# A transformer forward pass on one core: three mixer tiles on the unnormed input, and VectorE's convolution work in another order

## The reference

```python
hn = rmsnorm(h, norm_mix_g[l])        # (x * rsqrt(mean(x * x) + 1e-6)) * g
...
z = hn @ w_in                         # 1024 -> 2056 columns
za = jax.nn.gelu(z[..., :o0], approximate=False)
y_a = gmlp_spatial_gating(za[..., :D_A], za[..., D_A:], ln_a_g, ln_a_b, w_s, b_s)
zb = z[..., o0:o1]
y_b = conformer_conv(zb[..., :D_B], zb[..., D_B:], conv_b_w, conv_b_b, gn_b_g, gn_b_b)   # 31 taps
y_c = mlstm_group(z[..., o1:o2], z[..., o2:o3], z[..., o3:o4], z[..., o4:], ...)         # conv of 4 taps, 4 heads
return jnp.concatenate([y_a, y_b, y_c], axis=-1) @ w_out
```

## Time and profile before

| what | value |
|---|---|
| median of 3 runs | 1891.39 us (1889.86 to 1891.47) |
| the profiled execution's own time | 1891.13 us |
| its span, first to last instruction | 1889.3 us |
| PE busy | 1866.1 us |
| PE idle in the first 180 us | 11.4 + 1.1 + 0.7 us |
| mean granted TensorE clock | 0.998 |

### The profile page before, as it was taken

One profiled execution on the slowest core, in us unless ns is written; L12 is line 12 of the kernel. 1 busy time (PEld: TensorE's weight loads), 2 busy tenths in 40 slices (PEclk: granted clock), 3 DMA queues, 4 the chain that ended last, 5 costly groups with the idle time before them and its releaser, 6 DMA issues.

```text
span 1889.3 us, 24381 instructions
## 1 busy us (share of the span) xinstructions
PE 1866.1 (99%) x8998; PEld 1511.8 (80%) x8998; DVE 783.3 (41%) x1278; ACT 433.6 (23%) x846; POOL 1078.6 (57%) x622
## 2 busy tenths in 40 slices
PE   7999999999999999999999999999999999999998
PEld 5878887888888888876778888887877878888887
DVE  6774433352342433687451212127833561212123
ACT  5223422310010122156140101023424140101020
POOL 5755762576757656520556655565862546666652
PEclk9999999999999999999999999999999999999999
DMA  6322321232333224210223332222331223332331
GB/s 228 110 79 90 107 94 45 90 100 90 114 99 112 92 83 146 81 56 1 67 84 96 99 100 89 89 90 89 102 98 46 73 95 101 102 102 95 100 101 45
DMA packets 47455, 173.78 MB, mean 92 GB/s; under 512 B 5264, under 2 KB 5904, under 8 KB 46736
## 3 DMA queue, kind: packets, MB, share of 16 engines
q1 hardware_dynamic: 46800, 169.54, 28.0%
q10 hardware_dynamic: 576, 3.11, 0.5%
HBM read 170.53 MB, written 2.10 MB: 91 GB/s over the span
## 4 chain that ended last, share of the span: by engine, by line
PE 97%; DVE 1%; ACT 1%; DMA 0%; issue 0%; SPq 0%; DVEq 0%
PE acc L516 17%; PE acc L517 17%; PE acc L518 17%; PE acc L543 6%; PE acc L540 6%; PE acc L539 6%; PE acc L595 1%; PE acc L998 1%; PE acc L597 1%; PE acc L596 1%; PE misc L1014 1%; PE misc L1034 1%; PE acc L1190 1%; PE acc L1192 1%; PE acc L1191 1%; PE acc L615 1%
## 5 line engine op out<-in xcount | busy, mean ns | idle before, releaser
L2642 POOL TENSOR_SCALAR w_hi<-raw 128x1024 fp32r<-128x1024 f32 x309 | 335.0, 1084 | 757.9 <-PE acc L543 277.6
L2644 POOL TENSOR_TENSOR w_lo<-raw,w_hi 128x1024 fp32r<-128x1024 f32 x309 | 748.3, 2422 | 25.8
L516 PE MATMUL acc<-x_hi,w_hi 128*128 128x512 f32 x872 | 340.1, 390 | 0.0
L518 PE MATMUL acc<-x_hi,w_lo 128*128 128x512 f32 x872 | 339.3, 389 | 0.0
L517 PE MATMUL acc<-x_lo,w_hi 128*128 128x512 f32 x872 | 339.3, 389 | 0.0
L1970 DVE TENSOR_TENSOR h<-acc,h 128x512 f32<-128x512 f32 x112 | 77.4, 691 | 357.3 <-PE acc L518 226.5
L516 PE MATMUL acc<-y_hi,w_hi 128*128 128x512 f32 x540 | 211.3, 391 | 0.0
L518 PE MATMUL acc<-y_hi,w_lo 128*128 128x512 f32 x540 | 210.1, 389 | 0.0
L517 PE MATMUL acc<-y_lo,w_hi 128*128 128x512 f32 x540 | 210.1, 389 | 0.0
L516 PEld LDWEIGHTS acc<-x_hi,w_hi 128*128 128x128 f32 x872 | 163.7, 188 | 34.2 <-issue 0.3
L518 PEld LDWEIGHTS acc<-x_hi,w_lo 128*128 128x128 f32 x872 | 163.7, 188 | 34.0
(11 more groups left out here) (479 smaller groups left out, 2800.5 us busy)
## 6 DMA issues: line engine op xcount, KB each, us to landing
raw<-weights_dram SPq DMA_DIRECT2D x309, 512.0 KB, 3.5
h<-x_dram SPq DMA_DIRECT2D x2, 1024.0 KB, 6.3
out_dram<-out_tok SPq DMA_DIRECT2D x6, 256.0 KB, 2.1
small<-small_dram SPq DMA_DIRECT2D x1, 1408.0 KB, 15.9
mem_in<-mem_dram SPq DMA_DIRECT2D x1, 1024.0 KB, 13.0
w_cmp<-w_cmp_dram ACTq DMA_DIRECT2D x1, 1024.0 KB, 6.9
small<-small_dram ACTq DMA_DIRECT2D x1, 992.0 KB, 4.8
const<-const_dram SPq DMA_DIRECT2D x1, 640.0 KB, 9.2
```

What stands on the lines that cost most here:

```text
L516: mm(out, m["w_hi"][:, slot, k], hi[:, k], start=k == 0, stop=False)
L518: last = mm(out, m["w_lo"][:, slot, k], hi[:, k], start=False, stop=k == kc - 1)
L2642: nc.gpsimd.tensor_scalar(hi, m["raw"][:, slot], 1.0, 0.0, ALU.mult, ALU.add).then_inc(sem("weights_high"), 1)
L2644: nc.gpsimd.tensor_tensor(m["w_lo"][:, slot].rearrange("p k n -> p (k n)"), m["raw"][:, slot], bf(hi), ALU.subtract).then_inc(sem("weights ...
```

## The change

The first three tiles are now three of the four tiles of `xc`, and the tile of gate rows comes ninth. PE multiplies these three with `x * g`, which needs no norm: ACT writes its high part to `y_hi`, DVE its low part to `y_lo`, and DVE multiplies the finished banks by 1/rms (`r_late`) when it is there (`unnormed_out`). The first tile is split in two halves, and its first four chunks are multiplied before the second half is there. SP brings the first tile and the parameters ahead of x, and x in four pieces. Before that PE runs four products of ones. The sum of squares goes between the chunks of the third tile, behind the writing of `y_hi` and `y_lo` on ACT and DVE. `alpha_b` and `alpha_g` are written later.

DVE does the short convolution, the product of `b_in`, 5 of the 31 taps of the long one, the gate rows and masks, taps 5 to 26, the statistics of the values, two taps, the first head's diagonal, and the last two taps. The norm of the values takes 8 instructions where there were 12. PE takes `conv_mean` after `cell_out(0)` and `gating` after the scores of head 1; the small transposes of the rows stand behind the value tiles. The first head waits for `tile_out` 16 and no more for 17.

```diff
     gates = np.zeros((D, P), np.float32)
     gates[:, 0:4], gates[:, 32:36] = w_in[:, 2048:2052], w_in[:, 2052:2056]
+    for c in [8, 9, 10, 11, 6, 7, 4, 5]:
+        add(w_in, chunk(c))
     add(gates, slice(0, P))
-    for c in [8, 9, 10, 11, 6, 7, 4, 5, 12, 13, 14, 15]:
+    for c in [12, 13, 14, 15]:
         add(w_in, chunk(c))
     add_wide(w_in[:, 256:512], 256)
     for c in (0, 1):
...
-    pe.wait_ge(sem("const_in"), 16)
...
-    idle_products(1)
...
-    idle_products(2)
+    def unnormed(k, slots):
+
+        pe.wait_ge(sem("plain_high"), k + 1)
+        for slot in slots:
+            mm(acc[:, slot], m["w_hi"][:, slot, k], y_hi[:, k], start=k == 0, stop=False)
+            mm(acc[:, slot], m["w_lo"][:, slot, k], y_hi[:, k], start=False, stop=False)
+        pe.wait_ge(sem("plain_low"), k + 1)
+        for slot in slots:
+            last = mm(acc[:, slot], m["w_hi"][:, slot, k], y_lo[:, k], start=False, stop=k == KC - 1)
+            if k == KC - 1:
+                last.then_inc(sem("tile_done"), 1)
+
+    pe.wait_ge(sem("warm"), 1)
+    for _ in range(4):
+        mm(acc[:, 3], m["sum_h"][:, 0:P], m["sum_h"], start=True, stop=True)
+    pe.wait_ge(sem("first_half"), 1)
+    for k in range(HALF):
+        unnormed(k, (0,))
+    claim(0)
+    claim(1)
+    for k in range(HALF):
+        unnormed(k, (1,))
+    for k in range(HALF, KC):
+        unnormed(k, (0, 1))
+    claim(2)
+    for k in range(KC):
+        if k == 3:
+            pe.wait_ge(sem("const_in"), 16)
+            sum_squares("mix")
+        unnormed(k, (2,))
+
     def memory_norm(k):
         if k == 6:
             pe.wait_ge(sem("norm_rstd"), 1)
             sum_squares("mem", MEM)
 
-    pair_opening(0, x_hi, x_lo, "norm_high", "norm_ready", 0, 4, 0, memory_norm)
-    stage("mix_in", x_hi, x_lo, 10, at=3)
+    pair_opening(3, x_hi, x_lo, "norm_high", "norm_ready", 0, 3, 2, memory_norm)
+    stage("mix_in", x_hi, x_lo, 7, at=6)
+    tokens(13, 256, x_hi, x_lo, TB)
...
-    tokens(13, 256, x_hi, x_lo, TB)
     stage("mix_in", x_hi, x_lo, 2, at=15)
...
     def conv_mean(c):
-        pe.wait_ge(sem("conv_b"), c + 1)
-        mm(misc[:, 2 + c], pr.view("avg64"), m["conv_b"][:, c], start=True, stop=True).then_inc(sem("std_mean"), 1)
+        pe.wait_ge(sem("tap%d" % c), CONV_B)
+        mm(misc[:, c], pr.view("avg64"), m["conv_b"][:, c], start=True, stop=True).then_inc(sem("std_mean"), 1)
...
-        pe.wait_ge(sem("std_centred"), c + 1)
+        pe.wait_ge(sem("cell_norm"), 1)
...
         if head:
             pe.wait_ge(sem("p_c"), 4 * head)
+            pe.wait_ge(sem("std_centred"), 2)
...
@@ -773,8 +809,10 @@
 
         if head:
             pe.wait_ge(sem("cell_norm"), head)
+            pe.wait_ge(sem("y_a"), 2)
         else:
-            pe.wait_ge(sem("y_a"), 2)
+            for c in range(2):
+                pe.wait_ge(sem("tap%d" % c), CONV_B)
         pe.wait_ge(sem("p_c"), 4 * head + 4)
         for tb in range(TB):
             for sb in range(tb + 1):
@@ -790,23 +828,24 @@
             last = turn(acc[:, 3, blk(tb)], m["cell_tok"][:, tb], ident)
         last.then_inc(sem("cell_turned"), 1)
 
-    pe.wait_ge(sem("tile_out"), START["mem_kv"])
+    pe.wait_ge(sem("tile_out"), START["mem_kv"] - 1)
     pe.wait_ge(sem("row_cols_out"), 2)
     cell_in(0)
-    for c in range(2):
-        conv_mean(c)
     pe.wait_ge(sem("norm_ready"), chunks_before("mem") + KC)
     mem_k(0)
     cell_scores(0)
-    for c in range(2):
-        gating(c)
     mem_k(1)
     cell_out(0)
+    for c in range(2):
+        conv_mean(c)
     mem_v(0)
     for head in range(1, 4):
         cell_in(head)
         mem_k(2 * head)
         cell_scores(head)
+        if head == 1:
+            for c in range(2):
+                gating(c)
         mem_k(2 * head + 1)
         cell_turn(head - 1)
...
     logs()
+    act.wait_ge(sem("par_in"), 16)
     for k in range(KC):
-        act.wait_ge(sem("x_in%d" % (k // HALF)), 16)
+        act.wait_ge(sem("x_in%d" % (k // 2)), 16)
+        if k >= 2:
+            act.wait_ge(sem("plain_low"), k - 1)
+        own.link(f(pr.late_bank(k), m["h"][:, k], ACT.Copy, scale=pr.col("norm_mix_g", k)))
+        f(m["y_hi"][:, k], pr.late_bank(k), ACT.Copy).then_inc(sem("plain_high"), 1)
+    for k in range(KC):
         square("mix", k, m["h"])
-    rms_rstd("mix")
+    rstd, summed, _ = pr.norm_banks("mix")
+    act.wait_ge(sem("norm_summed"), 1)
+    rsqrt(m["r_late"], summed, 1.0 / D, RMS_EPS, "r_mix")
+    act.wait_ge(sem("r_mix"), 1)
+    f(rstd, m["r_late"], ACT.Copy).then_inc(sem("norm_rstd"), 1)
...
+    act.wait_ge(sem("tile_done"), 3)
+    rms_high("mem", m["mn_hi"], MEM)
+    act.wait_ge(sem("tile_out"), 3)
+    out(3, 3, m["xc"][:, 3, CONV_C - 1:])
+    for c in range(2):
+        out(4 + c, c, z[:, 2 + c], ACT.Sigmoid)
+    for c in range(4):
+        act.wait_ge(sem("xconv_pre"), c + 1)
+        f(m["xconv"][:, c], misc[:, c, :], ACT.Silu).then_inc(sem("xconv"), 1)
+    act.wait_ge(sem("tile_done"), 9)
+    act.wait_ge(sem("tile_out"), 8)
     own.mark(f(z[0:4, 0], acc[0:4, 0], ACT.Identity, bias=pr.col("b_igate", 0, 4)))
     fr, rt = z[0:4, 1], m["row_t"][0:4]
-    out(0, 0, fr, ACT.Identity, src=acc[32:36, 0], bias=pr.col("b_fgate", 0, 4))
...
+    out(8, 0, fr, ACT.Identity, src=acc[32:36, 0], bias=pr.col("b_fgate", 0, 4))
+    act.wait_ge(sem("tile_out"), 9)
...
@@ -1500,11 +1546,11 @@
     act.wait_ge(sem("v_a_stats"), 1)
     rsqrt(m["v_rstd"], m["v_mv"][:, :, 1], 1.0, LN_EPS, "v_a_rstd")
     mem_k(0)
+    weights_diagonal(0)
+    mem_k(1)
     for c in range(2):
         act.wait_ge(sem("std_centred"), c + 1)
         f(m["sq"][:, c], m["conv_b"][:, c], ACT.Square).then_inc(sem("std_sq"), 1)
-    weights_diagonal(0)
-    mem_k(1)
...
+    v.memset(m["sum_h"], 1.0).then_inc(sem("warm"), 1)
+    for k in range(KC):
+        dve.wait_ge(sem("plain_high"), k + 1)
+        v.tensor_tensor(m["y_lo"][:, k], pr.late_bank(k), bf(m["y_hi"][:, k]), ALU.subtract).then_inc(sem("plain_low"), 1)
     for k in range(1, KC):
         add_squares("mix", k)
...
-    dve.wait_ge(sem("par_in"), 16)
-    for j, bias in enumerate(("ln1_b", "ln2_b")):
-        own.mark(v.tensor_scalar(m["alpha_b"][:, blk(j, 16)], pr.view(bias), ALPHA, None, ALU.mult))
-    own.mark(v.tensor_scalar(m["alpha_g"], pr.view("final_g"), ALPHA, None, ALU.mult))
-    rms("mix", h, "norm_mix_g", m["x_hi"], m["x_lo"])
+
+    def unnormed_out(k):
+        if k in (0, 1, 3):
+            t = (0, 1, None, 2)[k]
+            dve.wait_ge(sem("tile_out"), t)
+            dve.wait_ge(sem("tile_done"), t + 1)
+            v.tensor_tensor(m["xc"][:, t, CONV_C - 1:], acc[:, t], m["r_late"], ALU.mult).then_inc(sem("tile_out"), 1)
+
+    dve.wait_ge(sem("r_mix"), 1)
+    rms("mix", h, "norm_mix_g", m["x_hi"], m["x_lo"], also=unnormed_out)
...
+    for c in range(2):
+        dve.wait_ge(sem("tile_out"), 6 + c)
+        dve.wait_ge(sem("tile_done"), 7 + c)
+        v.tensor_tensor(m["b_in"][:, c, CONV_B - 1:], acc[:, 2 + c], z[:, 2 + c], ALU.mult)\
+            .then_inc(sem("tile_out"), 1)
...
+    def long_taps(first, end):
+
+        for j in range(first, end):
+            for c in range(2):
+                if j:
+                    dve.wait_ge(sem("tap%d" % c), j)
+                conv_step(misc[:, 2 + c, :] if j < CONV_B - 1 else m["conv_b"][:, c], m["b_in"][:, c, j:j + S],
+                          pr.col("conv_b_w", 2 * j + c), pr.col("conv_b_b", c) if j == 0 else None, misc[:, 2 + c, :])\
+                    .then_inc(sem("tap%d" % c), 1)
...
+    def values_centred():
+
+        own.settle()
+        dve.wait_ge(sem("v_a_stats"), 1)
+        for tb in range(TB):
+            own.mark(v.scalar_tensor_tensor(vt[:, tb], vt[:, tb], mv[:, tb, 0:1], pr.view("ln_a_g"),
+                                            ALU.subtract, ALU.mult))
+
+    def values_normed():
...
+    def conv_centred():
+
         for c in range(2):
...
+            dve.wait_ge(sem("std_mean"), c + 1)
+            v.tensor_tensor(m["conv_b"][:, c], m["conv_b"][:, c], misc[:, c, :], ALU.subtract)\
+                .then_inc(sem("std_centred"), 1)
...
@@ -2141,6 +2202,8 @@
         own.settle()
         own.link(v.tensor_tensor(s, r, mv[:, :, 1], ALU.mult))
         v.tensor_tensor(s, s, r, ALU.mult).then_inc(sem("cell_var"), 1)
+        if head == 0:
+            conv_centred()
         if head < 3:
             cell_diagonal(head + 1)
...
+    dve.wait_ge(sem("tile_out"), 8)
+    dve.wait_ge(sem("xconv"), 4)
+    long_taps(0, 5)
+    rows()
+    long_taps(5, 27)
+    value_stats()
+    long_taps(27, 29)
     cell_diagonal(0)
-    dve.wait_ge(sem("tile_out"), START["mem_kv"])
-    gate(0)
+    own.link(v.memset(m["v_c"][:, :, P:], 1.0))
+    long_taps(29, CONV_B)
+    values_centred()
     cell_weights(0)
-    gate(1)
     cell_norm(0)
+    values_normed()
     for head in range(1, 4):
         cell_weights(head)
+        if head == 1:
+            gate(0)
+            gate(1)
```

(30 more changed lines are left out.)

121 lines of the change are left out of this document (40 added, 81 removed).

## The result

The change makes the kernel slower: 1893.53 us median (1892.51 to 1896.49, 12 runs) against 1889.91 us (12 runs of before beside them), ratio 1.0021, 95% interval 1.0013 to 1.0030. The forecast was 1885.9, range 1884.0 to 1889.2, and faster. The profiled execution took 1893.09 us, with a span of 1891.3 us, 2.0 more than before. From 170 us on the two traces run alike, so everything is decided in the mixer.

The account below looks back on a forecast made before the run. The prediction took PE to bound the kernel, busy 1866.1 us of a 1889.3 us span. Gains of 4.8 us at the start and 0.7 at the first head, 5.5 in all, took the 1891.39 median to 1885.9, range 1884.0 to 1889.2.

Parts of the forecast that it names:

- Centring the values, the same four: 116.7.: DVE before the first head's masked weights: four half-width instructions, at most 0.42 us each, end at 116.7 after 115.0.
- busy 69.8 us of 85.5: DVE from 32.0 to 117.5 in the earlier trace; the 69.8 us of work was carried over, from 43.5.
- Another four half-width instructions: Second half of the values' norm, behind the first head's norm; some 9 us of PE work stand ahead of the gating.
- I leave the 1.7 in both.: Around the gating: the clock's fall to 1.2 GHz for 3.4 us costs 1.7 us, before and after alike.
- Term 1: Start of the kernel: tile 5 is taken at 46.8 instead of 51.64, 4.8 us earlier.
- 0.17 MB more: First loads: extra bytes ahead of ACT's start, at 442 GB/s 0.4 us, so ACT begins at 6.4.
- signs of being wrong: Squares' chain starting after 17, granted clock under 1.00 between 7 and 20 us, or PE waiting for a tap or `std_centred`.
- Term 2: First head: its wait for the last `u_a` goes, 0.7 us gained; the head starts at 108.0.
- Rival 1: Clock falls at the start, 1887.3 us, or with a second fall at the gating, 1889.0; chance 0.12.
- Rival 2: VectorE late at the first head, its 100 instructions each 0.03 us longer: 1889.8, or 1888.0 if 3 late; chance 0.12.
- Rival 3: Start: the norm comes later than worked out, costing PE one for one, up to 1887.9 us; chance 0.10.
- Rival 4: Long convolution's taps no longer overlap, 11.8 us late on DVE: 5.4 us slower, 1896.8; chance 0.05.

Follow-up runs that it names:

- Experiment 4: Kernel after with only the second tensor of `values_centred` read from a PSUM bank, the norm's gain left out: 1891.74 us, ratio 1.0011.
- 2: Kernel after with `values_normed()` moved from behind `cell_norm(0)` into it, behind `conv_centred()`: 1888.97 us, ratio 0.9994.
- 5: Kernel after with `values_centred` and `values_normed` both reading their second tensor from PSUM, gain and bias left out: 1886.64 us, ratio 0.9983.
- 1: Kernel after with `cell_weights(0)` put ahead of `values_centred()` in DVE's order: 1891.38 us, ratio 1.0006.
- the first of 7: Kernel after with the parameters and two chunks of x loaded ahead of the first weight tile: 1896.03 us, ratio 1.0025.
- experiment 9: Kernel of experiment 3 with the parameters loaded behind all of x, the gain left out of the unnormed tiles: 1883.87 us, ratio 0.9970.
- Experiment 8: Kernel of experiment 3 with x loaded in two transfers of four chunks instead of four of two: 1887.42 us, ratio 0.9988.
- 10: Kernel of experiment 3, complete, with the loads of the parameters and the first two chunks of x exchanged: 1884.88 us, ratio 0.9975.
- experiment 3: Kernel after with `cell_weights(0)` ahead of `values_centred()` and `values_normed()` inside `cell_norm(0)`, run twice: 1885.51 and 1885.80 us, ratios 0.9979 and 0.9978.
- experiment 6: Kernel before with its twelve values' norm instructions replaced by the kernel after's eight, in the old place: 1890.43 us, ratio 1.0000.

## Why the prediction was wrong, step by step

**"Centring the values, the same four: 116.7."** This is the step that failed. It took 0.42 each from the earlier trace rows, from an instruction of the same width that reads one input from a PSUM bank (`misc`), and put the wait for GpSimd at nothing. PE was ready for `cell_out(0)` at 121.5, 1.7 late with all the rest (119.8 forecast). DVE came to the four at 118.64, 3.6 behind its forecast of 115.0, and they took 3.05 instead of 1.7; so the slack of 1.3 became a wait of 1.9. Experiment 4 shows the cause of the 3.05, two inputs in SBUF: the same place, the same form, one operand elsewhere, 1.65. The 0.5 of wait that is left there goes with DVE's late arrival. Of the 3.6 us, 1.7 are the late start, and nearly all the rest is one instruction of the gate rows, again with two inputs in SBUF beside GpSimd's work, which took 0.68 us in the kernel before:

```profile
78.09 2.70 DVE L2106 TENSOR_TENSOR row_em<-row_F,row_M 4x512 f32<-4x512 f32 x1
```

That it waited for GpSimd, whose `w_lo` runs from 77.08 to 80.25 there, was not tried by itself. The step "busy 69.8 us of 85.5" took DVE's work over as a fixed sum, whatever stood beside it, and so missed these 2.0 us.

**"Another four half-width instructions", with 9 us of PE ahead of the gating.** I gave them no time of their own and asked only whether PE had cover, not where DVE would stand. They came in front of head 1's masked weights, took 4.53 us, and PE waited 2.1 (experiments 2 and 5 remove it in two different ways). The prediction let the norm hide and said that a lost cover would cost under 1.5.

**The clock: "I leave the 1.7 in both."** It was 3.4 instead of 1.7. In the four kernels that waited 2.1 us before the gating (after, and experiments 1, 4 and the first of 7) the clock was at half for 3 to 10 us of the 40 from 120 to 160; of the ten profiled that did not wait there, eight never fell. The executions that were only timed agree: in these four kernels none of 43 had a mean clock above 0.998. That the wait brings the fall is borne out by these, not proved: before and experiment 9 fell without it. Nor was before's own 1.7 a constant: the times in the section on the result show that it comes in some executions only. The forecast took it from one execution, and set out from a median that had it, 1.5 us above the 1889.91 measured beside the kernel after.

**Term 1, 4.8 us.** The mechanism was right, its size 1.7 too large at the first head (109.70 against 108.0), and all of this is ScalarE's start: 8.08 against 6.4. The pace of 1.21 a chunk, eight pairs, the squares behind them, PE's wait of 1.3 and the chain to the memory's sum (43.71 against 42.0) came as worked out, each 1.7 to 1.9 late. The step that failed is "0.17 MB more", priced at 442 GB/s as 0.4 us, as if bytes at a steady rate decided when x is there. The rate was lower, 324 GB/s from 4 to 9 us, but that is not enough to explain it. ACT needed 0.52 + 0.17 + 0.52 = 1.22 MB, and these two windows (last: mean GB/s) make 1.23 MB by 5.70 us and 1.96 by 8.08:

```profile
0.00:5.70 5.70, 4.24 (x5) 1.85 (x6) 0.48 (x1) 1.28 (x1) 1.36 (x6) 1.00 0.67 215
0.00:8.08 8.08, 6.43 (x8) 2.50 (x8) 0.48 (x1) 1.28 (x2) 3.66 (x8) 1.00 0.76 242
```

So by 8.08 some 0.7 MB of later requests had been moved beside x. (In the kernel before it was 1.48 MB at 6.01, of which x is 1.05.) Experiment 8 speaks against the size of x's pieces, 9 and 10 point to the parameters' transfer, with one profiled execution each. What in it delays the rest (its rows of 1.3 KB, or its place) was not taken apart and stays open. Two of the prediction's own signs of being wrong came with it: the squares started at 17.78, after 17, and the clock fell between 7 and 20 us.

**Term 2, 0.7 us**, was right: no wait at the first head.

**The sum.** In the spans: 1.7 at the start, 1.9, 2.1 and 1.7 of clock are 7.4 of the 7.5 us between the 1883.8 forecast and the 1891.3 measured.

**The rivals.** Rival 1 came true at the gating, and at the start too, where PE worked at ACT's pace:

```profile
10.00:12.00 2.00, 2.00 (x6) 1.10 (x5) 0.96 (x3) 1.96 (x4) 1.19 (x2) 0.60 1.03 422
12.00:14.00 2.00, 2.00 (x6) 1.53 (x6) 1.23 (x2) 1.94 (x4) 2.00 (x1) 0.54 1.00 413
```

That fall cost nothing: PE's first product with `x_hi` stands at 30.50 with it, and at 30.52 in experiment 4, which had the same pace there and a clock of 1.00. The Trainium skill's "TensorE: Matmul & The Clock Gate" (section "HAM oscillation — how this bites in real kernels") was cited for it, bursts short against their waits. It bears on this place only loosely, since here the work (0.68 us in each 1.21) was longer than the pauses. The clock fell at this place in one execution and not in the other. Rival 2 came true by another cause: DVE was late, not by 100 instructions 0.03 longer but by a few that stood still. Rival 3 is the 1.7. Rival 4 did not happen: 44 taps took 29.04 us, 0.66 each. None of them alone gives 1893.5; it took three together, and the rival on the slow side was the wrong one. Its mechanism should have been DVE's two-input instructions beside GpSimd, and its rows were there to be read: before's norm of the values lay from 119.85 to 123.9, and POOL's pause from 116.56 to 122.27, behind which POOL took 2.54 us instead of 1.04.

## What to carry to other kernels

When a change moves VectorE instructions whose tensor inputs both lie in SBUF, look up what GpSimd does at the new place: price them by the GpSimd instruction that they may have to sit out, or give them one input in PSUM. Put whatever TensorE waits for ahead of them, and them into VectorE's own gaps; here two moved lines turned 0.2% slower into 0.2% faster. And don't price the first loads of a kernel by their bytes at a steady rate: here the first input came 1.7 us later than so worked out, and a small load ahead of it seems to have cost more than its bytes. Last, compare like with like: a kernel whose clock falls in some executions only has two times, some 1.6 us apart here, and a forecast has to say from which it starts.

## What the runs showed of the hardware

- VectorE instructions with two inputs in SBUF and GpSimd's split of a tile keep each other waiting. VectorE stood still behind GpSimd's 2.39 us subtraction (instructions of 1.86 and 2.56 us instead of 0.48) and behind its 1.19 us high part (1.26). GpSimd's high part took 1.19 us (kernel after, 137.41) and 1.29 (experiment 3, 128.19) instead of 1.04 when such an instruction was in progress. In the gate rows `row_em` took 2.70 us beside GpSimd (0.68 before). The Trainium skill's "SBUF — State Buffer" (section "SBUF: two separate sides") calls the port pair that the two engines share an exclusive lock, taken by a VectorE instruction with two SBUF inputs or by a GpSimd one, whichever starts first, while the other fully blocks. The traces agree for the `scalar_tensor_tensor` instructions, and 4.53 us for four of them is what it costs here.
- Who waits also hung on the form. A GpSimd instruction that started at 122.27 in the kernel before took 2.54 us, and four `tensor_tensor` that started after it went ahead at 0.42 each. With `scalar_tensor_tensor` in their place (experiment 6) GpSimd's took 1.33 and VectorE's one 1.26. For a row of `tensor_tensor`, "whichever starts first" does not hold in these traces.
- One input in PSUM is enough to escape it: 1.65 us for four beside the same GpSimd instruction. Of the 60 taps of 128x512 in the kernel after, 48 ran beside a GpSimd instruction, and all took 0.72 to 0.75 us, 0.66 from one start to the next.
- The same loads landed at different times in different executions: ScalarE's first chunk stood between 6.98 and 8.10 us in seven profiled kernels with the same order of the first loads, and TensorE's first `x_hi` product 22.4 to 22.5 us behind it in each.
- A TensorE wait of 2.1 us was followed in all four profiled cases by 3 to 10 us at 1.2 GHz. Taking the wait away in experiment 2 gave 4.6 us, more than twice its length. But the clock fell for 3.4 us in the kernel before as well, at a place without any wait, and by the mean clocks only in some executions (41 of 103).
